# Last mixer of a two-model kernel: compressed outputs added by TensorE onto the turned outputs of a group

## The reference, cut to what matters

```
s_c = einsum('bqhgd,bchd->bqhgc', qq, k_cmp)          # 15 compressed keys
p_c = masked_softmax(s_c, cmp_end <= t)
o_c = einsum('bqhgc,bchd->bqhgd', p_c, v_cmp)
...                                                    # o_s: selected blocks, o_w: window
return gb[...,0]*o_c + gb[...,1]*o_s + gb[...,2]*o_w   # then: o @ w_out
```

## Time and profile before

| what | value |
|---|---|
| median of 3 runs | 1930.35 us (1929.79 to 1930.58) |
| the profiled execution | 1928.99 us |
| its span, first to last instruction | 1927.0 us |
| TensorE busy | 1916.8 us |
| VectorE busy | 1187.6 us |
| ScalarE busy | 1183.9 us |
| GpSimd busy | 405.9 us |
| the last mixer's unit loop | about 1652 to 1719 us of the span |

### The profile page before, as it was taken

The page is one execution under the profiler, slowest core; times in us unless marked ns, Lnnn a source line. Parts: engine busy times, 40 slices in busy tenths (PEclk is TensorE's granted clock), DMA queues, the critical chain, the costliest instruction groups (busy, mean ns, idle before and its releaser), DMA issues.

```text
span 1927.0 us, 26845 instructions
## 1 busy us (share of the span) xinstructions
PE 1916.8 (99%) x9488; PEld 1616.0 (84%) x9488; DVE 1187.6 (62%) x1639; ACT 1183.9 (61%) x2113; POOL 405.9 (21%) x749
## 2 busy tenths in 40 slices
PE   9999999999999999999999999999999999999999
PEld 7888988888888898888888898888888888888887
DVE  6555656556655666555755657655576555876554
ACT  7555557555655666555755546755587555756553
POOL 1222302221322102221322101222112221201221
PEclk9999999999999999999999999999999999999999
DMA  9657436664655426665555444655557553306650
GB/s 331 216 189 208 153 110 204 190 195 152 221 189 185 151 76 217 199 192 179 182 194 192 165 142 134 216 196 196 175 174 235 188 196 125 110 23 219 196 196 23
DMA packets 241056, 338.80 MB, mean 176 GB/s; under 512 B 5727, under 2 KB 206478, under 8 KB 240830
## 3 DMA queue, kind: packets, MB, share of 16 engines
q1 hardware_dynamic: 239710, 335.68, 53.3%
q0 software_dynamic: 496, 1.23, 0.3%
q10 hardware_dynamic: 752, 0.61, 0.1%
HBM read 336.45 MB, written 1.05 MB: 175 GB/s over the span
## 4 chain that ended last, share of the span: by engine, by line
PE 96%; DVE 1%; ACT 1%; issue 0%; POOL 0%; DMA 0%; SPq 0%; ACTq 0%; DVEq 0%
PE A L545 11%; PE A L547 11%; PE A L546 11%; PE G L545 10%; PE G L547 10%; PE G L546 10%; PE X L545 8%; PE X L546 8%; PE X L547 8%; PE A L1275 2%; PE A L958 1%; PE X L1259 1%; PE G L1287 1%; DVE wl L506 0%; POOL work L816 0%
## 5 line engine op out<-in xcount | busy, mean ns | idle before, releaser
L506 DVE TENSOR_TENSOR wl<-raw,wh 128x1024 fp32r<-128x1024 f32 (+1 forms) x553 | 658.3, 1230 | 132.7 <-ACT wh L497 131.7
L497 ACT ACTIVATE wh<-raw 128x1024 fp32r<-128x1024 f32 (+1 forms) x553 | 556.0, 1052 | 175.7 <-PE G L547 71.5
L816 POOL COPY work<-work 32x128 f32<-32x128 f32 x640 | 323.6, 506 | 909.1 <-DVE work L2566 885.8
L545 PE MATMUL G<-wh,xh 128*128 128x512 f32 (+1 forms) x814 | 317.8, 390 | 0.3
L547 PE MATMUL G<-wh,xl 128*128 128x512 f32 (+1 forms) x814 | 316.3, 389 | 0.0
L546 PE MATMUL G<-wl,xh 128*128 128x512 f32 (+1 forms) x814 | 316.1, 388 | 0.0
L545 PE MATMUL X<-wh,xh 128*128 128x512 f32 x672 | 261.7, 389 | 1.1 <-DVE wl L506 1.1
L547 PE MATMUL X<-wh,xl 128*128 128x512 f32 x672 | 261.5, 389 | 0.0
L546 PE MATMUL X<-wl,xh 128*128 128x512 f32 x672 | 261.4, 389 | 0.0
L1908 ACT ACTIVATE work<-work 32x128 f32<-32x128 f32 x640 | 196.4, 307 | 16.4 <-DVE work L2566 9.9
L2571 DVE TENSOR_TENSOR hidl<-work,hidh 128x512 fp32r<-128x512 f32 x80 | 55.4, 692 | 237.4 <-ACT hidh L1914 237.4
(11 more groups left out here) (497 smaller groups left out, 2928.5 us busy)
## 6 DMA issues: line engine op xcount, KB each, us to landing
raw<-in_ffn_w_in SPq DMA_DIRECT2D x88, 1024.0 KB, 6.8
raw<-in_ffn_w_down SPq DMA_DIRECT2D x44, 1024.0 KB, 5.0
raw<-in_ffn_w_out SPq DMA_DIRECT2D x44, 1024.0 KB, 4.9
raw<-in_ffn_w_gate SPq DMA_DIRECT2D x42, 1024.0 KB, 5.5
raw<-in_ffn_w_up SPq DMA_DIRECT2D x42, 1024.0 KB, 7.3
raw<-in_a_w_in SPq DMA_DIRECT2D x12, 1024.0 KB, 5.4
raw<-in_ab_w_in SPq DMA_DIRECT2D x8, 1024.0 KB, 6.9
raw<-in_kv_w SPq DMA_DIRECT2D x6, 1024.0 KB, 5.2
```

The lines of the kernel that those rows point to most:

```text
L497: nc.scalar.activation(hi, r, ACT.Copy).then_inc(hi_done[u], 1)
L506: nc.vector.tensor_tensor(lo, r, hi.bitcast(F32), ALU.subtract).then_inc(lo_done[u], 1)
L545: nc.tensor.matmul(o, sh, rh, start=start, stop=False)
L816: last = nc.gpsimd.tensor_copy(*square_views(i, j))
```

## The change

The compressed product is not made at the end of its group any more. The turned probabilities stay in SBUF, in a place of their own for each group (`cPT` becomes a list of four). When the outputs of a group are turned, the four turns open an accumulation in the bank, and two matmuls add the compressed outputs onto it, already turned: the values `vC` are now the side that stays in the array (two heads, 128 columns) and `cPT` (256 tokens) the side that streams. The product in bank `A[3]`, ScalarE's copy of it and VectorE's additions are gone, with the events `nsa_oc`, `nsa_oc_out` and `nsa_added`. The turn of a group now waits for `nsa_summed`, which its last `combine` sets. `compressed_scores` takes over the wait for `nsa_pc_out`, which frees bank `A[2]`; VectorE's part of it waits for `nsa_pc_turned` where it waited for `nsa_oc`.

```diff
--- before.py
+++ after.py
@@ -443,7 +443,7 @@
                    blk=cut(work, 0, 16, 60), hk4=cut(work, 1024, 2, NKV, 4, CP), ksw=cut(work, 1024, NT, 8, HD),
                    qd=cut(arena, 0, 16, 2, HD), q=cut(arena, 3712, NT, D), g=cut(arena, 5760, NT, 48),
                    sq=cut(arena, 6112, NT, 4, HD), sq0=cut(arena, 6624, NT, 4, HD), pc=cut(arena, 5856, NT, 4, CP),
-                   cPT=cut(arena, 3216, NT, P), tmp=cut(work, 2048, 4, HD), o=y[:],
+                   cPT=[cut(arena, at, NT * P) for at in (3216, 6624, 6880, 6112)], tmp=cut(work, 2048, 4, HD), o=y[:],
                    ss=cut(st, pair_at, 32), ms=cut(st, pair_at + 32, 32), rs=stat(32))
         k_gain = nsa["rs"][:, 20:23]
         lane_max = nmax.rearrange("p a t n -> p (a t n)").rearrange("p (u l) -> p u l", l=4)
@@ -1693,8 +1693,6 @@
                     pe.wait_ge(event("nsa_qd"), 2 * kvg + 2)
                     if kvg:
                         pe.wait_ge(event("nsa_pl"), kvg)
-                    if kvg >= 2:
-                        pe.wait_ge(event("nsa_oc_out"), kvg - 1)
                     for b in range(2):
                         for a in range(2):
                             for t in range(NT):
@@ -1741,6 +1739,8 @@
 
                 def compressed_scores(kvg):
 
+                    if kvg:
+                        pe.wait_ge(event("nsa_pc_out"), kvg)
                     mm(A[2][:, 0:S].rearrange("p (t h c) -> p t h c", t=NT, c=CP), ident_r,
                        cmp_mask_r.rearrange("p (t c) -> p t c", t=NT).unsqueeze(2).to_broadcast([P, NT, 4, CP]), start=True,
                        stop=False)
@@ -1762,20 +1762,19 @@
                                                    nsa["pc"][:, t, :, :].rearrange("p h c -> p (h c)"), ident)
                     last.then_inc(event("nsa_pc_turned"), 1)
 
-                def compressed_values(kvg):
-
+                def turn_group(kvg):
+
+                    pe.wait_ge(event("nsa_summed"), kvg + 1)
                     pe.wait_ge(event("nsa_pc_out"), kvg + 1)
-                    if kvg + 1 == NKV:
-                        pe.wait_ge(event("nsa_oc_out"), kvg)
-                    for t in range(NT):
-                        last = mm(A[3][:, t * S:(t + 1) * S], nsa["cPT"][:, t, :],
-                                  nsa["vC"][:, kvg, :, :].rearrange("p h n -> p (h n)"), start=True, stop=True)
-                    last.then_inc(event("nsa_oc"), 1)
-
-                def turn_group(kvg):
-
-                    pe.wait_ge(event("nsa_added"), kvg + 1)
-                    turn_pair(nsa["o"], kvg)
+                    for i in range(2):
+                        c = 2 * kvg + i
+                        for t in range(NT):
+                            mm(TB[kvg][:, i * S + t * P:i * S + (t + 1) * P], nsa["o"][:, t, c * P:(c + 1) * P], ident,
+                               start=i + t == 0, stop=False, is_transpose=True)
+                    for i in range(2):
+                        two = nsa["vC"][:, kvg, 2 * i:2 * i + 2, :].rearrange("p h n -> p (h n)")
+                        last = mm(TB[kvg][:, i * S:(i + 1) * S], two, nsa["cPT"][kvg], start=False, stop=i == 1)
+                    last.then_inc(o_turned, 1)
 
                 turn_queries(0)
                 small_sums("nsa_g", A[1], (6, 7, 4, 5))
@@ -1791,8 +1790,6 @@
                         scores_lo(n + 2).then_inc(unit_s, 1)
                     elif n + 2 < UNITS["nsa"]:
                         scores(n + 2)
-                    if n >= 0 and j == 5 and kvg + 1 < NKV:
-                        compressed_values(kvg)
                     if j == 5 and kvg + 1 < NKV:
                         compressed_scores(kvg + 1)
                     if n == -1:
@@ -2403,11 +2399,6 @@
                         for t in range(NT):
                             last = A_(nsa["g"][:, t, :], A[0][:, 48 * t:48 * (t + 1)], ACT.Exp, scale=rstd[:, t:t + 1])
                         last.then_inc(event("nsa_gates"), 1)
-                    if n >= 0 and j == 5 and kvg + 1 < NKV:
-                        act.wait_ge(event("nsa_oc"), kvg + 1)
-                        if kvg:
-                            act.wait_ge(event("nsa_added"), kvg)
-                        A_(nsa["sq0"].rearrange("p t h n -> p (t h n)"), A[3][:, :], ACT.Copy).then_inc(event("nsa_oc_out"), 1)
                     if n >= 0:
                         turned_out("nsa", n)
                     if n >= 0 and j == 0:
@@ -2419,7 +2410,7 @@
                         queries_hi(kvg + 1)
                     if n >= 0 and j == 4:
                         act.wait_ge(event("nsa_pc_turned"), kvg + 1)
-                        A_(nsa["cPT"], A[2][:, 0:S].rearrange("p (t n) -> p t n", t=NT), ACT.Copy
+                        A_(nsa["cPT"][kvg], A[2][:, 0:S], ACT.Copy
                            ).then_inc(event("nsa_pc_out"), 1)
                 split_out("nsa", KC)
                 prep("nsa", 4, (1,))
@@ -3181,7 +3172,7 @@
 
                     dve.wait_ge(event("nsa_sc"), kvg + 1)
                     if kvg:
-                        dve.wait_ge(event("nsa_oc"), kvg)
+                        dve.wait_ge(event("nsa_pc_turned"), kvg)
                     src = A[2][:, 0:S].rearrange("p (t h c) -> p t h c", t=NT, c=CP)
                     if kvg == 0:
                         link(V.tensor_tensor(pc, src, wide(nsa["rs"][:, 0:8].rearrange("p (t h) -> p t h", t=NT).unsqueeze(3),
@@ -3198,19 +3189,6 @@
                     link(V.reciprocal(rs, ms))
                     r = rs.rearrange("p (t h) -> p t h", t=NT)
                     V.tensor_tensor(r, r, g[:, :, 4 * kvg:4 * kvg + 4], ALU.mult).then_inc(event("nsa_pz"), 1)
-
-                def add_compressed(kvg):
-
-                    dve.wait_ge(event("nsa_oc_out"), kvg + 1)
-                    part = nsa["o"][:, :, S * kvg:S * (kvg + 1)]
-                    V.tensor_tensor(part, part, nsa["sq0"].rearrange("p t h n -> p t (h n)"), ALU.add
-                                    ).then_inc(event("nsa_added"), 1)
-
-                def add_last(t):
-
-                    dve.wait_ge(event("nsa_oc"), NKV)
-                    part = nsa["o"][:, t, S * (NKV - 1):S * NKV]
-                    return V.tensor_tensor(part, part, A[3][:, t * S:(t + 1) * S], ALU.add)
 
                 def queries_lo(kvg):
 
@@ -3236,7 +3214,12 @@
                                     ).then_inc(unit_n, 1)
                     dve.wait_ge(unit_n, BASE["nsa"] + n + 1)
                     part = nsa["o"][:, t, HD * heads[0]:HD * (heads[0] + nh)].rearrange("p (h n) -> p h n", n=HD)
-                    link(V.tensor_tensor(part, tmp[:, :, 0, :], tmp[:, :, 1, :], ALU.add))
+                    last = V.tensor_tensor(part, tmp[:, :, 0, :], tmp[:, :, 1, :], ALU.add)
+                    if n % NSA_GROUP == NSA_GROUP - 1:
+                        last.then_inc(event("nsa_summed"), 1)
+                        dve.wait_ge(event("nsa_summed"), n // NSA_GROUP + 1)
+                    else:
+                        link(last)
 
                 queries_lo(0)
                 query_sums(1)
@@ -3254,17 +3237,12 @@
                         queries_lo(kvg + 1)
                     if n == 3 or n > NSA_GROUP and j == 2:
                         compressed_probs(kvg)
-                    if n > NSA_GROUP and j == 3:
-                        add_compressed(kvg - 1)
                     if n == UNITS["nsa"] - 1:
-                        add_last(1)
                         split_out("nsa", KC, (0, 2))
                     if n == UNITS["nsa"]:
                         split_out("nsa", KC, (1, 3))
                     if n >= 1:
                         combine(n - 1)
-                    if n == UNITS["nsa"]:
-                        add_last(0).then_inc(event("nsa_added"), 1)
                 split_out("nsa", KC, OUT_ORDER[4:])
                 prep("nsa", 4, (1,))
                 prep("nsa", 5, (1,))
```

## The result

The changed kernel takes 1933.09 us (median of 20 runs, 1930.91 to 1935.42) against 1929.83 us (20 runs, 1929.42 to 1930.58): ratio 1.0016, interval 1.0010 to 1.0022. It is 3.3 us slower; I had forecast 1929.9 and a range to 1932.1. (The forecast was a gain of 0.44 us counted from the 1930.35 of three runs; from the 1929.83 of twenty it would have been 1929.4.) The spread of the runs has grown from 1.2 us to 4.5. One execution in this document, of the last experiment, ran at a clock of 0.752 throughout (2388.75 us) and is left out of what is said of that experiment.

What follows compares the result with a forecast made beforehand. TensorE, busy 99% of the span at full clock, was taken as the bound; -2.88 (loop) + 2.61 (end) - 0.17 (projection wait) = -0.44 us gave 1929.9 us against 1930.35, range 1927.9 to 1932.1.

Steps and rivals of the forecast that it cites:

- TensorE's work moved, not changed: Compressed products: same size and count; three pairs leave the loop (-2.88 us) and come in at the end (+2.61 us).
- The waits stay: Unit loop: TensorE's 2.35 us of waits, such as 0.30 and 0.44 us before late scores, remain; VectorE's and ScalarE's relief credited nothing.
- the zero taken for the lost cover: Group boundaries: removing 0.96 us of cover opens no new wait; taken as zero, bounds -2.35 to +2.9 us.
- The chain: Within a group: query turns, ScalarE's copy, VectorE's subtraction, maxima, exponentials, scores; begins and ends on TensorE, 5.37 us apart.
- The end: Mixer's end: turns and products before the output projection, which starts 1.8 us later; small wait before its second part covered, -0.17 us.
- the gap: Output projection: its second part waited 0.17 us for chunk 1; forecast to be covered, -0.17 us.
- VectorE's queue: Mixer's end: unit 23's combination has 1.9 us to spare; in the second rival, ending a whole combination late gives 1931.0 us.
- the accumulating turn: End: turns left open for an added product might take two records each, +1.7 us, 1931.6 us; part of the second rival.
- the second rival: Mixer's end: accumulating turns cost more (1931.6 us) or VectorE's queue bites (1931.0 us); chance 0.10.
- the clock: Rival, loop or end: TensorE drops to 1.2 GHz, costing 5.7 us (1935.6) or 17 per group; decides from 3.9 us; chance 0.03.
- -2.88 + 2.61 - 0.17: Forecast sum: products leaving the loop, products entering the end, and the projection's covered wait, -0.44 us together.
- the rule weighed in the prediction: Trainium skill, TensorE turns: transposes do not count as busy for the full clock; by it the sum would be a loss.

Runs made afterwards that it cites:

- e10: The last experiment: e7's kernel with the query turns of groups 1 and 2 moved ahead of their step's values; 1928.93 us, stretch 107.86.
- e9: Changed kernel with the compressed scores parted into four runs of four matmuls over two steps; 1933.67 us, stretch 112.23.
- e1: Changed kernel with the six loop products back at their old place, unused; 1932.11 us, clock 1.000 in all eleven runs.
- e3: Changed kernel with eight unused turns of 128 columns at each of the three places where two products stood; 1932.02 us, clock 1.000.
- e4: Kernel before the change with the compressed products of groups 0, 1 and 2 left out; 1930.37 us, clock 0.998 or 0.999 in all eleven runs.
- e5: Changed kernel with the low-half eight of the sixteen 32-column matmuls moved behind that step's values; 1930.28 us, eight runs at clock 1.000, three below.
- e7: Changed kernel with the eight low-half 32-column matmuls one step later, behind that step's wide scores; 1930.93 us, on a second set of runs 1930.44.

## Why the prediction was wrong

- **TensorE's work moved, not changed.** Right: equal record counts, 0.85 us out of each boundary (0.96 forecast; the mask takes 0.23 us there and not the 0.12 of the first group), 0.87 into the end three times; with the clock held, the edit alone is -0.25 to -0.3 us in the mixer (-0.44 forecast).
- **The waits stay.** Right in the trace: the zero taken for the lost cover holds for waits. The chain given for them is right for the first wait of each pair and not for the second, by e10.
- **The end.** Right, a little too small: with the gap went 0.30 us and not 0.17. VectorE's queue held nothing up, and the accumulating turn costs no more than a plain one (0.44 us for four): the second rival is out.
- **The step that failed** is the clock, which has no term in the sum: -2.88 + 2.61 - 0.17 takes TensorE at full clock on both sides. Where the prediction weighs the cover taken from the boundary ("I take zero for this") it asks whether any engine would be waited for, and never what TensorE's own clock would do with what is left there. The clock stood among the rivals at 0.03, and "against it" was read from the clock row of the page and from idle time. Neither bears on it: the first is too coarse to show even the fall that happened, and e9 has twice the idle time at full clock.
- **What the runs showed in its place:** without the products in the loop the clock fell, 3.4 us lost over 7 us, so -0.5 + 3.4 = +2.9 in the mixer and 3.3 in the medians. With products or turns back it held (e1, e3), and in the kernel before it fell once they were taken out (e4).
- **The rival's price and reason** were not right either. It priced 5.7 us for the end or 17 for a group; 3.4 were lost. Its 3.9 us only marks where a loss would count as slower. It blamed turns "with fewer matmuls between them"; but turns hold the clock (e3), and it fell behind the 32-column matmuls. So the rule weighed in the prediction, which spoke against the change, had its direction right by luck.
- Whether the kernel before stood near the edge is open. Of the 100 runs of it taken beside the experiments 14 read 0.999, but none of those has a trace, and the fall may be at the program's start as in e5.

## What to carry to other kernels

Before taking matmuls from a stretch, look at what stays: in this kernel matmuls of 32 or 65 columns, which take 0.10 us each where a turn of 128 takes 0.11, keep the profile's PE at 100%, and with enough of them in a row the granted clock fell all the same. Here the wide work or the turns between them paid for themselves. Read the clock in windows of 2 us around the place, since a page's row hides a fall of 7 us. Where thin matmuls must be, part them, as far as the engine that consumes them can bear it: in halves it cost no time in the mixer here (e7), in quarters 3.6 us (e9). Compare small edits by a stretch between two fixed points, since the start of the program differed by 1.8 us between traces.

## What was not expected of the hardware

- TensorE's clock fell from 2.4 to 1.2 GHz while TensorE was 100% busy in the records, and came back after about 7 us in the changed kernel, with TensorE at work throughout.
- 2.6 us of useless products, or as many useless turns, made the changed kernel 1.0 us faster; nearly the same busy time in 65-column products made it 3.7 us slower.
- An fp32 turn that opens an accumulation, with a product added on it, takes the one record and the 0.11 us of any other turn here.
